# Hybrid encoder step on one core: last weighted sum of a block behind the next logits, an output strip loaded before the late modulation columns, one more first group on VectorE

## What is computed

```python
for l in range(DEPTH):                                   # DEPTH = 2
    mod = silu(c) @ w_ada[l] + b_ada[l]                  # 6 x 1024 columns: shift, scale, gate, twice
    h = rmsnorm(x, g_norm1[l]) * (1.0 + sc1) + sh1
    z = h @ w_in[l]                                      # columns shared out to three mixers
    a_out = chunk_gmlp_mixer(...)
    b_out = sparse_attention_mixer(...)                  # score, top 256 keys, softmax, weighted sum
    c_out = conformer_conv_mixer(...)
    x = x + ga1 * (concatenate([a_out, b_out, c_out]) @ w_out[l])
    h2 = rmsnorm(x, g_norm2[l]) * (1.0 + sc2) + sh2
    x = x + ga2 * ((silu(h2 @ w_gate[l]) * (h2 @ w_up[l])) @ w_down[l])
```

## Time and profile before

| | us |
|---|---|
| median of 3 runs | 3079.72 |
| the 3 runs | 3079.29, 3079.72, 3083.76 |
| the profiled execution's own time | 3078.23 |
| its span, first to last instruction | 3076.5 |
| attention of layer 0, first logits to search end | 399 to 577 |
| attention of layer 1, the same | 1909 to 2090 |
| PE busy over the span | 92% |
| granted TensorE clock, mean | 0.965 of full speed |

### The profile page before, as it was taken

How to read it: one execution, slowest core, us unless ns; L and a number is a source line. 1 busy time by engine, 2 the same in 40 slices (tenths; PEclk the granted TensorE clock), 3 DMA queues, 4 the chain that set the end, 5 groups by cost and what they waited for, 6 DMA issues and landing times.

```text
span 3076.5 us, 42656 instructions
## 1 busy us (share of the span) xinstructions
PE 2845.4 (92%) x16018; PEld 2455.6 (80%) x16018; DVE 1652.3 (54%) x2788; ACT 988.1 (32%) x1261; POOL 617.1 (20%) x262
## 2 busy tenths in 40 slices
PE   5999778979999999999979987889999999999996
PEld 2778633349999999999977875333999999999996
DVE  6767766784443444434545678564435335353355
ACT  4246546422321111111233564563332111111112
POOL 1411300001122122221242122000111222322221
PEclk9999989979999999999989998999999999999998
DMA  5412100151222212222241311002012222222222
GB/s 213 134 63 83 36 21 1 42 197 44 69 85 66 87 64 86 81 69 89 64 143 42 116 51 36 1 1 63 28 55 89 70 80 81 69 89 70 80 81 85
DMA packets 71351, 224.93 MB, mean 73 GB/s; under 512 B 17232, under 2 KB 17488, under 8 KB 70096
## 3 DMA queue, kind: packets, MB, share of 16 engines
q1 hardware_dynamic: 69664, 217.26, 20.9%
q10 hardware_dynamic: 1584, 6.29, 0.5%
HBM read 211.44 MB, written 11.54 MB: 72 GB/s over the span
## 4 chain that ended last, share of the span: by engine, by line
issue 46%; PE 34%; DVE 6%; ACT 6%; POOL 4%; DVEq 2%; DMA 1%; ACTq 0%; POOLq 0%; SPq 0%
PE ps L930 32%; ACT notsel L734 4%; POOL w_lo L587 4%; PE ps L976 1%; DVE hf L1322 1%; DMA w_ada<-in_w_ada 1%; DVEq L1447 1%; DVE ada_later L1341 1%; DVE ada_junk L1341 0%; PE ps L956 0%; PE ps L1037 0%; DVE swapped L1412 0%; DVE s_cand L1445 0%; PE ps L912 0%; DVEq L1351 0%
## 5 line engine op out<-in xcount | busy, mean ns | idle before, releaser
L587 POOL TENSOR_TENSOR w_lo<-w_raw,w_hi 128x1024 fp32r<-128x1024 f32 x202 | 497.7, 2464 | 2344.6 <-ACT w_hi L686 2344.6
L930 PE MATMUL ps<-u_hi,w_hi 128*128 128x352 f32 (+1 forms) x2112 | 457.5, 325 | 2.1 <-ACT rstd L881 2.1
L930 PE MATMUL ps<-u_hi,w_lo 128*128 128x352 f32 (+1 forms) x2112 | 458.4, 325 | 0.0
L930 PE MATMUL ps<-u_lo,w_hi 128*128 128x352 f32 (+1 forms) x2112 | 455.7, 324 | 0.0
L686 ACT CAST w_hi<-w_raw 128x1024 fp32r<-128x1024 f32 x202 | 211.1, 1045 | 548.1 <-PE ps L930 323.4
L930 PEld LDWEIGHTS ps<-u_hi,w_hi 128*128 128x128 f32 x2112 | 362.1, 189 | 3.7 <-ACT rstd L881 2.7
L930 PEld LDWEIGHTS ps<-u_lo,w_hi 128*128 128x128 f32 x2112 | 361.0, 189 | 0.0
L930 PEld LDWEIGHTS ps<-u_hi,w_lo 128*128 128x128 f32 x2112 | 360.9, 189 | 0.0
L734 ACT ACTIVATE notsel<-score,s_cand 128x384 bf16<-128x384 f32 (+3 forms) x248 | 297.4, 1200 | 142.1 <-DVE s_cand L1445 141.8
L1758 DVE SCALAR_TENSOR_TENSOR x<-ps,mod,x 128x704 f32 (+2 forms) x240 | 125.4, 578 | 364.3 <-PE ps L930 358.5
L930 PE MATMUL ps<-a_hi,w_hi 128*128 128x352 f32 x1056 | 228.7, 325 | 4.2 <-DVE x L1758 2.1
(11 more groups left out here) (261 smaller groups left out, 4119.6 us busy)
## 6 DMA issues: line engine op xcount, KB each, us to landing
w_ada<-in_w_ada SPq DMA_DIRECT2D x96, 512.0 KB, 4.8
w_raw<-in_w_up SPq DMA_DIRECT2D x88, 512.0 KB, 3.4
w_raw<-in_w_in SPq DMA_DIRECT2D x34, 512.0 KB, 3.6
ada_later<-in_w_ada SPq DMA_DIRECT2D x32, 512.0 KB, 3.5
cw<-in_convw SPq DMA_DIRECT2D x32, 512.0 KB, 4.5
w_raw<-in_w_down SPq DMA_DIRECT2D x32, 384.0 KB, 3.2
w_raw<-in_w_down SPq DMA_DIRECT2D x32, 320.0 KB, 2.9
w_raw<-in_w_out SPq DMA_DIRECT2D x16, 512.0 KB, 3.4
```

The lines of the kernel that those rows point to most:

```text
L587: nc.gpsimd.tensor_tensor(w_lo[slot][:], w_raw[:], w_hi[slot][:].bitcast(F32), ALU.subtract)\
L930: last = nc.tensor.matmul(ps[:, bank + t, 0:w], wt[slot][:, kk, :], mv[:, kk, t * TW:t * TW + w], start=(at == 0 and p == 0), stop=(at == ...
```

## The change

Four things, in code order.

`ADA_PE, ADA_DVE` go from 3, 1 to 2, 2: two loads of four column groups on each side. SP's queue gets a second load of 2 MB behind the first one, ACT's loses its third.

In SP's list output strip 1 is loaded right behind the cached values (`vcache`) and ahead of the later modulation columns; the two halves of `x` then follow one another. In layer 1 the order stays as it was.

On PE the weighted sum of a unit is made one unit of `ORDER` later, whatever kind that unit is. Within a block that is as before. At a block's end the last `pv` stood directly behind the one before it; now it stands behind the next unit, which is the first L unit of block i+2 (behind unit S of block i, the list goes on with the L units of i+2), and for block 6 the first S unit of block 7. The last one of all stays last. ACT's and DVE's lists in attention ("counts where they are") are the same.

In layer 0 DVE makes 13 later columns ahead of the output of block 7 and 11 behind the maxima of the sample; `modulation` of slots 2 to 5 moves behind the sample's output.

```diff
-ADA_PE, ADA_DVE = 3, 1
+ADA_PE, ADA_DVE = 2, 2
...
-            sp.dma_start(w_ada0[0][:], a["w_ada"][DEPTH - 1, 4 * ADA_PE:ADA_FIRST].rearrange("m p k -> p m k")).then_inc(ada0_loaded[0].sem, 16)
+            for n in range(ADA_DVE):
+                m = 4 * (ADA_PE + n)
+                sp.dma_start(w_ada0[n][:], a["w_ada"][DEPTH - 1, m:m + 4].rearrange("m p k -> p m k")).then_inc(ada0_loaded[n].sem, 16)
...
                     sp.dma_start(vcache[:, :, n, 0:HD], a["vcache"][l, :, :, n]).then_inc(kv_cached.sem, 16)
+                load_strip(FIRST_OUT + 1, a["w_out"][l, 1])
                 if l == 0:
                     load_later(ADA_STRIPS + 3, 48 - ADA_FIRST)
                     sp.wait_ge(later_used.sem, 48 - ADA_FIRST)
                     for d in range(4):
                         bring_back(d)
-                for j in range(1, OUT_STRIPS):
+                sp.wait_ge(c_ready.sem, c_ready.at(l, 2))
+                settle(sp)
+                for d in range(4, KD):
+                    bring_back(d)
+                for j in range(2, OUT_STRIPS):
                     load_strip(FIRST_OUT + j, a["w_out"][l, j])
-                    if j == 1:
-                        sp.wait_ge(c_ready.sem, c_ready.at(l, 2))
-                        settle(sp)
-                        for d in range(4, KD):
-                            bring_back(d)
...
+                late = None
                 for kind, n in ORDER:
                     if kind == "L":
                         logits(n)
-                        continue
-                    st(n)
-                    i, kb = S_UNITS[n]
-                    if kb >= 1:
-                        pv(n - 1)
-                    if kb == i:
-                        pv(n)
+                    else:
+                        st(n)
+                    if late is not None:
+                        pv(late)
+                    late = n if kind == "S" else None
+                pv(late)
...
-            dve.wait_ge(ada0_loaded[0].sem, 16)
-            for e in range(4):
-                modulate(w_ada0[0][:, e], 4 * ADA_PE + e)
-                dve.drain()
+            for n in range(ADA_DVE):
+                dve.wait_ge(ada0_loaded[n].sem, 16)
+                for e in range(4):
+                    modulate(w_ada0[n][:, e], 4 * (ADA_PE + n) + e)
+                    dve.drain()
...
-                half = ADA_STRIPS + (48 - ADA_FIRST - ADA_STRIPS) // 2
+                half = ADA_STRIPS + 13
                 output(QB - 2, 2, P, (QB - 2) * P, (QB - 1) * P)
...
                 if l == 0:
                     modulate_later(half, 48 - ADA_FIRST)
-                    modulation(l, 1, 2, 6)
                 mixed_lo(M_LOW[1:2])
                 output(QB, 3, DEC, SEQ, TOK)
+                if l == 0:
+                    modulation(l, 1, 2, 6)
                 mixed_lo(M_LOW[2:])
```

More of the change, by code:

```diff
@@ L703, in _ @@
             for n in range(ADA_PE):
-                act.dma_start(w_ada0[1 + n][:], a["w_ada0"][4 * n:4 * n + 4].rearrange("m p k -> p m k")).then_inc(ada0_loaded[1 + n].sem, 16)
+                act.dma_start(w_ada0[ADA_DVE + n][:], a["w_ada0"][4 * n:4 * n + 4].rearrange("m p k -> p m k"))\
+                    .then_inc(ada0_loaded[ADA_DVE + n].sem, 16)
             act.wait_ge(consts_made.sem, 1)
@@ L951, in _ @@
             for n in range(ADA_PE):
-                pe.wait_ge(ada0_loaded[1 + n].sem, 16)
+                pe.wait_ge(ada0_loaded[ADA_DVE + n].sem, 16)
                 if n >= 2:
@@ L956, in _ @@
                     last = nc.tensor.matmul(ps[0:2, n % 2, :], cond[:, kk, :],
-                                            w_ada0[1 + n][:, :, kk * P:(kk + 1) * P],
+                                            w_ada0[ADA_DVE + n][:, :, kk * P:(kk + 1) * P],
                                             start=(kk == 0), stop=(kk == KD - 1))
```

## The result

The changed kernel takes 3092.3 us (median of 8 executions, 3090.9 to 3096.7); the kernel before, on the same chip, 3082.6 (8 executions, 3079.3 to 3084.1). The ratio is 1.0036, interval 1.0027 to 1.0046: slower by 11 us (8 to 14); the two medians lie 9.7 us apart. The forecast was +9.4, which on the median of 3079.7 known then gave 3089.1.

What follows compares the result with a forecast made beforehand. Bounds: PE from layer 0's output projection on; in attention the chain of last sum, reciprocals, count, decision and maxima. Start -2.8, layer 0 +1.5 and layer 1 +10.7 gave +9.4 us, so 3089.1 us, range 3083 to 3095.

Steps and rivals of the forecast that it cites:

- the late sums: Attention: each block's last weighted sum behind the next unit delays reciprocals, counts and decisions, +10.7 us per layer.
- Start, -2.8: Start: PE has one column group less, DVE ends its groups sooner, first `hf` at 54.3, 2.8 us sooner.
- The first gap, -1.1 per layer: Attention's start: block 2's first L unit fills PE's wait for the first exponential, 1.1 us less per layer.
- End of block 2, to a total of +4.0: Attention: the L unit ahead of the moved sum waits for DVE's selection; reciprocals come later, total delay +4.0 us.
- Ends of blocks 3, 4 and 5, +1.6, +1.6, +1.4: Attention: each moved sum stands behind an L unit, +1.6 us; block 5's is partly taken up by DVE's second maximum.
- First decisions: Attention: DVE's first decision of each block would wait 2 to 4 us for ACT's count.
- End of block 6, +2.1 and +1.8: Attention: the last sum stands behind block 7's first S unit, +2.1 us on DVE, +1.8 on PE.
- Layer 0, net +1.5: Head of layer 0's output projection: the earlier strip load saves 9 us, attention gives them back, net +1.5 us.
- Layer 1, +10.7: Layer 1 passes attention's whole delay on to the end, +10.7 us.
- the clock rival: PE's new gaps in attention bring its lower clock: 5 us more for both layers, 3094 us; chance 16%.
- That attention hides the later reciprocals: Rival: decisions have 1.6 us or more of slack, so PE's order costs nothing: -14 us, 3065.7; chance 10%.
- Half of it: Rival: only the selection's wait and the last block's pass, +5.6 us per layer, sum -0.5, 3079 us; chance 14%.

Runs made afterwards that it cites:

- e4: The kernel before with only the first modulation groups split 2, 2 in place of 3, 1: 3077.8 us, ratio 0.9988.
- e11: e10 with the last weighted sum of block 0 alone put behind the next unit: 3075.4 us, ratio 0.9979 to the kernel before.
- e1: The changed kernel with each block's last weighted sum back directly behind the one before it: 3071.3 us, ratio 0.9962 to the kernel before.
- e13: The changed kernel with matmuls on constants in PE's wait ahead of the first sums of blocks 1 to 6: 3088.3 us, ratio 1.0027 to before.
- e9: The changed kernel with the moved last sum kept at the end of block 2 alone: 3076.5 us, one execution.
- e5b: The changed kernel with the moved last sum kept at the end of block 6 alone: 3072.8 us, one execution.
- e3: The kernel before with only SP's order changed, strip 1 loaded ahead of the later columns: 3073.6 us, ratio 0.9973.
- e10: e1 with 12 and 12 later modulation columns in place of 13 and 11: 3068.8 us, one execution.
- e2: The kernel before with only PE's order changed, each weighted sum one unit later: 3109.0 us, ratio 1.0082.
- e7: e1 with each block's first count ahead of the reciprocals on ACT: 3071.1 us, ratio 0.9967 to the kernel before.
- e12: e7 with matmuls on constants in PE's wait ahead of the first sums of blocks 1 to 6: 3057.5 us, ratio 0.9922 to before.

## Why the prediction was right, point by point

By the ratios the late sums cost 22.8 us (25.3 alone) for a forecast 21.4, the strip gave 8.3 for 9.2 (10.7 less 1.5), and the first groups 3.7 for 2.8. Sign and make-up of the sum are shown by these runs. That it came within 2 us is partly luck, since each part is known to 3 to 5 us only, and the misses of the strip and of the first groups, 0.9 each, cancel. One pair of profiles is a poorer witness: there the changed kernel is 1.85 us ahead at the first exponential, loses 2.7 by the second addition to `x`, gains 3.0 in the stretch where nothing was changed and loses 15.2 in layer 1, 13 us in all.

**Start, -2.8.** `hf` at 53.64 for a forecast 54.3; e4 gives -3.7 (interval -6.5 to -0.9). I had DVE's last group stretched by POOL's `w_lo` to 53.1, and that was wrong: its operation took 1.22 us as ever, and POOL's took 2.92 in place of 2.34. The small operations behind it were the ones that stalled again (1.90), and `hf` came 0.7 sooner than forecast. The Trainium skill (SBUF — State Buffer, section Who interferes with whom) has DVE and GpSimd exclude each other at a shared pair of ports, and issue order decide which of them waits. The rows agree: DVE's large operation began at 49.68, ahead of POOL's at 50.19, and POOL's became 0.58 us longer; DVE's small ones began at 51.32, behind POOL's, and were through at 53.22, when POOL's was (53.11). They stalled that long because POOL's began 1.0 us later than forecast (49.2): `find_rstd` ahead of it ended at 49.2 and not at 48.1.

**The first gap, -1.1 per layer.** It was filled, and the first reciprocals came 1.2 us sooner where PE was slow and 0.5 later where it had been fast (3.10 in the earlier trace rows's profile, 3.63 after). As a gain in time it did not show: e11, the only run with it alone, is not faster than e1. This term should have been 0 at best.

**End of block 2, to a total of +4.0.** In layer 0 of the kernel before every sum up to there was fast, and the reciprocals stood 39.5 us behind the first exponential. They stand at 44.8 in the changed kernel, +5.3, and with fillers (e13) at 43.8 and 43.3 in the two layers, +4.4 and +3.9. So the term was right, and the rest is the sum of block 2 at the lower clock. The wait for the selection is right in layer 1, in e9 and in e13; in layer 0 of the changed kernel PE's clock stood in for it.

**Ends of blocks 3, 4 and 5, +1.6, +1.6, +1.4.** Between the reciprocals of one block and the next the changed kernel has 1.8, 1.6 and 1.6 us more than e1 in layer 0, and 1.6, 1.6 and 1.7 in layer 1: the second maximum took up nothing. The last count, forecast +8.6 without the start's gain, stands 10.5 and 10.2 us later than before in the two layers, against the layer's first exponential, and 8.4 and 8.7 later than in e1. Which of the two is nearer to 8.6 is luck of the clock: e1, with nothing changed in attention, is itself 2.1 and 1.5 us behind the kernel before, most of it in layer 0 by the first sum of block 0 (1.98 us before, 3.68 in e1).

**First decisions.** I had them wait 2 to 4 us; they wait 4.68, 3.12, 2.54, 1.95 and 1.36. That DVE would come sooner to the first of them, since the L unit no longer stands behind the sum, I had not seen.

**End of block 6, +2.1 and +1.8.** e5b: +2.0, with a wait of PE of 1.59.

**Layer 0, net +1.5.** The cast at 688.48 was forecast for 688.7, but that figure had the start's gain left out, so the nearness is luck. Against the layer's first exponential DVE's output of block 6 stands 10.9 us later (forecast 10.7), the cast 4.0 later (forecast 2.4), the first addition 5.0 and the second 2.7 (forecast 0.6 to 2.4). e3 gives -8.3 for the strip, with -9 forecast. The step by which 13 and 11 columns cost nothing was wrong by 0.5 to 0.7 us: DVE waits 2.00 us for PE where it waits 0.62 in the kernel before and 0.92 in e10.

**Layer 1, +10.7.** Too small: against the layer's first exponential DVE's output of block 6 stands 13.4 us later than before, and the first addition 15.2. Behind the output of block 7 nothing was changed in this layer, and still the cast comes 34.3 us behind it where it came 32.2: PE was granted 0.62 of its clock in the 20 us from 2158, against 0.74 at the same place before (from 2147). This is the clock rival, given 16% and 5 us for both layers. In e13's profile 8 us of layer 1 are gone (276.8 us from first exponential to first addition, 268.9 with fillers) and only 0.5 of layer 0, but that is the fastest of e13's nine executions, 3.1 us under their median; by the medians fillers take away 3 to 4, which is not clear of noise. So part of the rival's 5 us may be in the result, and the runs don't settle how much. That 3092.3 lies above the forecast 3089.1 says nothing for it: the median of the kernel before is 2.9 us higher as well.

**The rivals that fell.** That attention hides the later reciprocals (10%): every first decision waited longer. Half of it (14%): e2 shows 25 us for two layers, not 11.

## What to carry to other kernels

Before an engine's last step of a group is put behind other work, follow its result through the next queues: here 1.6 us on PE were 1.6 us on ACT, on a count that had nothing to do with the sum, and on the search, at each of the ends of blocks 3, 4 and 5, and more where PE had to wait for a selection ahead of the moved sum. Reordering that queue (the count ahead of the operation that waits) gave back nearly all of it (21.6 us) without touching PE. Where PE waits again and again for other engines, look at its clock at each restart as well. In the old order of sums, taking away the waits of the decisions (e1 to e7) gave nothing by itself, and matmuls on constants in PE's waits then gave 13.6 us; in the changed order the same ones gave 3 to 4 at most. A wait is not a price, either: the engine that waits may just have come sooner.

## What the runs showed of the hardware

The clock at a restart isn't settled by the wait ahead of it. Ahead of block 0's first sum PE waits 1.11 us in every kernel that has the old order there; the four matmuls then took 1.98 us in 12 of 18 places and 3.63 to 3.70 in 6. The same row in e4_first_groups_alone:

```profile
417.36 3.63 PE L1180 MATMUL ps<-probs,vaug 128*128 128x512 f32 x4 [1.11 <-ACT probs L840]
```

The slowest such sums took 3.75 us for the same four matmuls that take 1.88 elsewhere, a factor of two, as between 1.2 and 2.4 GHz. The Trainium skill (TensorE: Matmul & The Clock Gate, section HAM oscillation — how this bites in real kernels) describes waits that bring the lower clock back each time, in a loop of the same step. Here it was one time in three for the shortest of the waits, and in e1_old_sums, which waits 3.12 us ahead of block 2's sum in layer 0, the sum took 1.95. With more than half of each of these waits filled (1.02 us left ahead of block 2's sum, from 2.41 in e7) no first sum behind block 1 was slow in either layer of e12.

A stretch in which nothing was changed still differs from one profile to the next: from the second addition to `x` of layer 0 to the first exponential of layer 1 (712 to 1927 in the changed kernel) it took between 1214.5 and 1219.8 us in the fourteen profiles here. Differences of 2 or 3 us in where a layer starts say nothing of a change; distances within a layer do.
